# Five of nine output tiles summed on TensorE and scaled by ScalarE and GpSimd, in a new final order

## The chip, the core and the metric

The kernel runs on one core of a Trainium2 chip. The metric is the device time of one launch in microseconds, the median of several runs. Every engine has its own instruction stream and waits for others by semaphores: TensorE (PE, with its weight loads as PEld), VectorE (DVE), ScalarE (ACT), GpSimd (POOL) and SyncE (SP), which here issues nearly all the large DMAs.

## The reference: what is computed

One layer of a decoder trunk for 1024 prompt tokens and 64 sample tokens of 1024 features, all in float32. First come three parallel branches fed by one input projection, a gated sum of them and an output projection; then a mixture of experts in which each token goes to the two best of eight experts in its best group; last a normalisation. What the change touches is the last step for each token:

```python
xn2 = rmsnorm(x, n2)
x = x + hier_moe(xn2...)          # two expert outputs per token, each times its gate
...
def rmsnorm(x, g):
    y = x * rsqrt(mean(x * x) + EPS)
    return y * g
y_prompt = rmsnorm(xp, final_norm_g)
y_sample = rmsnorm(xs, final_norm_g)
```

So for each token: the residual row, plus gate 0 times the first expert's row, plus gate 1 times the second's, then the sum scaled by the inverse root of its mean square and by the gain vector.

## The kernel before

The 1088 tokens are nine tiles: 0 to 7 have 128 rows, tile 8 (the sample tokens) has 64. The program is one stream for each engine, written by hand; there is no scheduler, so that the order of the code is the order on the engine.

The first two thirds are the projections and branches (`group`, lines 2009 to 2011, three products for each to keep float32's precision). Then follow the 64 experts: their weights stream in from memory, TensorE multiplies, and GpSimd scatters each expert's rows to `ytok` in device memory (`scatter`, line 1079), so that every token finds its two rows there.

The change lies in what comes behind the last expert, which this document calls the tail. SP waits until all scatters have landed and issues nine reads, one for each tile in the order of the list `FINAL` (`load_c`, line 881); each brings both expert rows of each token into the tile's own buffer `FY[n]` (1 MB, 0.5 MB for tile 8). Then SP issues nine stores in the same order, each behind a wait for its tile (`store_c`, line 890). Reads and stores go out on one queue.

The sum of a tile is made in one of two ways:

- a tile in `WEIGHED` on TensorE: `residual` (line 2368) multiplies the residual tile `X2` by the identity into two banks of PSUM, `weigh` (line 2375) adds the two expert rows, each multiplied by a diagonal matrix `GD` of the gates. PSUM has eight banks and a tile takes two, so four tiles fit at a time. Semaphore `c_mm` tells of the sum.
- any other tile (`SUMMED`) on VectorE: `combine` (line 1970), two `scalar_tensor_tensor`, each followed by a drain, with the sum left in `X2`. Semaphore `c_sum`.

ScalarE then squares and adds up the row (`norm_f`, line 1418) and takes the root (line 1420, `c_rms`); VectorE takes the reciprocal (`norm_out`). The scaling is made in one of two ways:

- a tile in `SCALED`: ScalarE multiplies by the reciprocal (`scale_f`, line 1425, `c_scaled`), GpSimd by the gain (`gain`, line 1124, `c_gained`);
- any other (`ON_DVE`): one `scalar_tensor_tensor` on VectorE does both (line 1986, `c_out`).

ScalarE's stream puts `scale_f` of a tile behind `norm_f` of the tile that follows it in `FINAL`; VectorE's puts `norm_out` of a tile behind `combine` of the one that follows. These two rules and the lists below set the order of the tail.

```python
FINAL = [0, 3, 1, 4, 2, 5, 8, 6, 7]
WEIGHED = [3, 4, 5, 6]
SCALED = [0, 1, 2]
```

Of the kernel before, what the change touches and what calls it, by code (L numbers as in the profile page):

```python
# [9 lines left out]
ACT = mybir.ActivationFunctionType  # L10
# [10 lines left out]
NT = NFULL + 1  # L21
# [32 lines left out]
def rows_of(tile):  # L54
    return P if tile < NFULL else NDEC


def trunk(nc, x_prompt, x_sample, state_conv, state_gla, norm1_g, w_in, conv_w, gla_a2, gla_a_b,
# [17 lines left out]
    with ctx:  # L76
# [10 lines left out]
        ident = keep("ident", [P, P])  # L87
        epsc = keep("epsc", [P, 1])
# [157 lines left out]
        X2 = sb("X2", [P, NT, D])  # L246
# [84 lines left out]
        GD, = place(OH_AT, [("GD", [P, 5, 2, P])])  # L331
# [83 lines left out]
        c_mm, c_sum, c_rms, c_out, c_st = sem("c_weighted"), sem("c_sum"), sem("c_rms"), sem("c_out"), sem("c_stored")  # L415

        c_root, c_scaled, c_gained = (rms_ready, NT), (xh_ready, NT), (xl_ready, NT)
# [44 lines left out]
                eng.drain().then_inc(s_over, 1)  # L462
                eng.wait_ge(s_over, 10)

        FINAL = [0, 3, 1, 4, 2, 5, 8, 6, 7]
        WEIGHED = [3, 4, 5, 6]
        SCALED = [0, 1, 2]
        SUMMED = [n for n in FINAL if n not in WEIGHED]
        ON_DVE = [n for n in FINAL if n not in SCALED]
        T_COL = [C_V + CW * i for i in range(4)] + [C_R + CW * i for i in range(4)] + [C_VV, C_VV + CW]  # L470
        NTC = len(T_COL)
        W_R, W_LR, W_VV = 4, 7, 8
# [131 lines left out]
        def _(sp):  # L604
# [7 lines left out]
            def load_w(w):  # L612
# [287 lines left out]
        def _(pool):  # L900
# [220 lines left out]
            def gain(i):  # L1121
                out = FY[SCALED[i]][:, 0, :]
                pool.wait_ge(c_scaled[0], c_scaled[1] + i + 1)
                pool.tensor_tensor(out, out, gfb[:], ALU.mult).then_inc(c_gained[0], 1)
            pool.wait_ge(r4_in, 112)
            for i in range(len(SCALED)):
                gain(i)
# [4 lines left out]
        def _(act):  # L1132
# [276 lines left out]
            def norm_f(n):  # L1409
                rows = rows_of(n)  # L1410
                if n in WEIGHED:
                    i = WEIGHED.index(n)
                    act.wait_ge(c_mm, i + 1)
                    x2 = ps[0:rows, 2 * i:2 * i + 2, :].rearrange("p b n -> p (b n)")
                else:
                    act.wait_ge(c_sum, SUMMED.index(n) + 1)
                    x2 = X2[0:rows, n, :]
                act.activation(jf[0:rows], x2, ACT.Square, accum_out=ss6[n][0:rows])
                act.drain()
                act.activation(rt6[n][0:rows], ss6[n][0:rows], ACT.Sqrt, bias=epsc[0:rows], scale=1.0 / D).then_inc(c_rms, 1)  # L1420

            def scale_f(n):
                i = SCALED.index(n)
                act.wait_ge(c_root[0], c_root[1] + i + 1)
                act.activation(FY[n][:, 0, :], X2[:, n, :], ACT.Copy, scale=rs6[n][:]).then_inc(c_scaled[0], 1)
            for i, n in enumerate(FINAL):
                norm_f(n)
                if i and FINAL[i - 1] in SCALED:
                    scale_f(FINAL[i - 1])
# [4 lines left out]
        def _(dve):  # L1434
# [467 lines left out]
            def gate_diagonals(n):  # L1902
                rows = rows_of(n)
                i = WEIGHED.index(n)
                for k in range(2):
# [21 lines left out]
            def expert(st):  # L1927
# [22 lines left out]
                if st.n == 22:  # L1950
                    over_count()
                if st.n - 24 in WEIGHED:
                    gate_diagonals(st.n - 24)
# [20 lines left out]
            def norm_out(n):  # L1974
                rows, x2 = rows_of(n), X2[0:rows_of(n), n, :]
                dve.wait_ge(c_rms, FINAL.index(n) + 1)
                if n in SCALED:
                    dve.reciprocal(rs6[n][0:rows], rt6[n][0:rows]).then_inc(c_root[0], 1)
                    return
                dve.reciprocal(rs6[n][0:rows], rt6[n][0:rows])  # L1980
                dve.drain()
                if n in WEIGHED:
                    bank = 2 * WEIGHED.index(n)
                    dve.wait_ge(c_mm, WEIGHED.index(n) + 1)
                    x2 = ps[0:rows, bank:bank + 2, :].rearrange("p b n -> p (b n)")
                dve.scalar_tensor_tensor(out=FY[n][0:rows, 0, :], in0=x2, scalar=rs6[n][0:rows], in1=gfb[0:rows], op0=ALU.mult, op1=ALU.mult).then_inc(c_out, 1)
            for i, n in enumerate(FINAL):
                if n in SUMMED:
# [8 lines left out]
        def _(pe):  # L1997
# [48 lines left out]
            for tile in range(NT):  # L2046
                rows = rows_of(tile)
                last = pe.transpose(ps[0:LOWRANK, 4 + tile // 3, tile % 3 * P:tile % 3 * P + rows], AT[0:rows, tile, :], ident[0:rows, 0:rows])
# [313 lines left out]
                y_mul(st)  # L2362
            overflow(pe, blocks_over(pe), again)

            def residual(i):
                n, rows = WEIGHED[i], rows_of(WEIGHED[i])
                for b in range(2):
                    pe.matmul(ps[0:rows, 2 * i + b, :], ident[0:rows, 0:rows], X2[0:rows, n, b * 512:(b + 1) * 512], start=True, stop=False)

            def weigh(i):  # L2370
                n, rows = WEIGHED[i], rows_of(WEIGHED[i])
                pe.wait_ge(cy_in[n][0], cy_in[n][1] + 16)
                for b in range(2):
                    for k in range(2):
                        last = pe.matmul(ps[0:rows, 2 * i + b, :], GD[0:rows, i, k, 0:rows], FY[n][0:rows, k, b * 512:(b + 1) * 512], start=False, stop=(k == 1))
                last.then_inc(c_mm, 1)
            pe.wait_ge(y_ready, NE)
            residual(0)
            residual(1)
            for i in range(len(WEIGHED)):  # L2380
                weigh(i)
                if i + 2 < len(WEIGHED):
                    residual(i + 2)
            barrier(pe, 1)


# [26 lines left out]
```

## Time and profile before

| what | us |
|---|---|
| median of 3 runs | 1862.06 (1861.51 to 1862.4) |
| the profiled execution's own time | 1861.46 |
| its span, first to last instruction | 1859.5 |
| TensorE busy in it | 1759.5 (95%) |
| VectorE, ScalarE, GpSimd busy | 584.6, 449.3, 240.2 |
| tail: from the first read of `ytok` (1820.0) to the end | 39.5 |

The profile's page gives the busy time of each engine and the chain of work that ended last; 95% for TensorE is an average over the whole program. The tail is the last 2% of the span, and it has to be read by itself: which engine waits for which, when the reads of `ytok` land, and whether the DMA engines stand still at some point. Times in the rows count from the span's start. In a row of the timeline, the bracket at the end is the idle time of the engine before the first instruction of the row and what ended it.

### The profile page before, as it was taken

To read this page: it belongs to the slowest core of one execution; us is meant where nothing else is said; L and a number is where in the kernel's file an instruction comes from. 1 tells how busy PE (TensorE), PEld (TensorE's weight loads), DVE (VectorE), ACT (ScalarE), POOL (GpSimd) and SP (SyncE) were. 2 spreads that over 40 slices of the span, in tenths; PEclk is the share of its full clock that TensorE was granted. 3 is DMA by queue.
4 is the path that set the end of the run, shared out by engine and by line. 5 is a ranking of instruction groups with operands and counts; after the bars stand their busy time and mean duration, and the time that the engine had idled before them with its cause. 6 is when DMAs were issued, how large, how long until landed. Compare 5 with 4: busy or idle time off the path is not lost.

```text
span 1859.5 us, 27679 instructions
## 1 busy us (share of the span) xinstructions
PE 1759.5 (95%) x11544; PEld 1475.4 (79%) x11544; DVE 584.6 (31%) x1076; ACT 449.3 (24%) x802; POOL 240.2 (13%) x297
## 2 busy tenths in 40 slices
PE   8999999999999999999999999999899888888885
PEld 8999999999888888899999998887655545544442
DVE  5000102432233322255214436655333111111115
ACT  6221225632223222231122104211111111111113
POOL 0003210000001101000000000000332222222221
PEclk9999999999999999999999999999999999999998
DMA  4232223244435535267616435244899999999997
GB/s 157 94 94 96 70 85 126 95 151 141 127 114 180 167 117 169 102 215 259 227 43 236 142 94 196 93 159 161 348 421 424 425 424 424 424 425 424 424 376 294
DMA packets 159479, 406.34 MB, mean 219 GB/s; under 512 B 20342, under 2 KB 102134, under 8 KB 134779
## 3 DMA queue, kind: packets, MB, share of 16 engines
q1 hardware_dynamic: 137402, 344.22, 49.6%
q0 software_dynamic: 21952, 60.34, 8.3%
q8 instruction: 93, 1.52, 0.3%
q14 instruction: 32, 0.25, 0.0%
HBM read 340.62 MB, written 79.60 MB: 226 GB/s over the span
## 4 chain that ended last, share of the span: by engine, by line
PE 90%; issue 4%; DVE 2%; DMA 2%; ACT 1%; DVEq 0%; SPq 0%; ACTq 0%; POOLq 0%
PE ps L2009 17%; PE ps L2011 16%; PE ps L2010 16%; PE ps L2314 12%; PE ps L2207 8%; PE ps L2336 6%; PE ps L2301 2%; PE ps L2315 1%; PE ps L2325 1%; PE ps L2098 1%; PE ps L2108 1%; PE ps L2109 1%; DMA FY<-ytok 1%; PE ps L2022 1%; PE ps L2244 1%
## 5 line engine op out<-in xcount | busy, mean ns | idle before, releaser
L2009 PE MATMUL ps<-XH,WH 128*128 128x384 f32 (+1 forms) x1152 | 382.6, 332 | 0.0
L2011 PE MATMUL ps<-XH,WL 128*128 128x384 f32 (+1 forms) x1152 | 376.9, 327 | 0.0
L2010 PE MATMUL ps<-XL,WH 128*128 128x384 f32 (+1 forms) x1152 | 376.8, 327 | 0.0
L2314 PE MATMUL ps<-E,yt 128*64 128x256 f32 x1024 | 248.3, 398 | 58.8 <-issue 57.7
L2315 PE MATMUL ps<-E,yt 128*64 128x256 f32 x1024 | 249.4, 400 | 0.0
L2314 PEld LDWEIGHTS ps<-E,yt 128*64 128x64 f32 x1024 | 141.6, 143 | 120.8 <-issue 65.3
L2009 PEld LDWEIGHTS ps<-XH,WH 128*128 128x128 f32 x1152 | 216.1, 188 | 17.0 <-issue 15.1
L2010 PEld LDWEIGHTS ps<-XL,WH 128*128 128x128 f32 x1152 | 216.4, 188 | 0.0
L2011 PEld LDWEIGHTS ps<-XH,WL 128*128 128x128 f32 x1152 | 216.2, 188 | 0.0
L2009 PE MATMUL ps<-WH,XH 128*128 128x256 f32 (+2 forms) x648 | 184.3, 284 | 4.6 <-DVE XL L1450 4.6
L1456 DVE TENSOR_TENSOR WL<-RAW,WH 128x2048 fp32r<-128x2048 f32 (+1 forms) x34 | 78.1, 2298 | 347.8 <-ACT WH L1156 347.7
L2010 PE MATMUL ps<-WL,XH 128*128 128x256 f32 (+2 forms) x648 | 183.6, 283 | 0.0
L2011 PE MATMUL ps<-WH,XL 128*128 128x256 f32 (+2 forms) x648 | 183.4, 283 | 0.0
L1196 ACT ACTIVATE OF<-ps 128x384 f32<-128x384 f32 (+1 forms) x120 | 56.8, 473 | 368.8 <-PE ps L2011 368.7
L2315 PEld LDWEIGHTS ps<-E,yt 128*64 128x64 f32 x1024 | 141.8, 143 | 0.0
L2009 PEld LDWEIGHTS ps<-WH,XH 128*128 128x128 f32 (+1 forms) x648 | 122.7, 189 | 6.4 <-issue 5.6
L2336 PE MATMUL ps<-E,HT 128*64 128x512 f32 x512 | 124.0, 605 | 1.1 <-DVE HT L1924 1.1
L2011 PEld LDWEIGHTS ps<-WH,XL 128*128 128x128 f32 (+1 forms) x648 | 122.9, 190 | 0.0
L1918 DVE TENSOR_TENSOR hid<-ps,sil 64x256 f32<-64x256 f32 x64 | 26.7, 417 | 303.8 <-ACT sil L1383 303.8
L2010 PEld LDWEIGHTS ps<-WL,XH 128*128 128x128 f32 (+1 forms) x648 | 122.0, 188 | 0.0
L1079 POOL DMA_INDIRECT ytok<-YS,yidx x64 | 65.2, 1019 | 352.6 <-ACT YS L1390 352.6
L1383 ACT ACTIVATE sil<-ps 64x256 f32<-64x256 f32 x64 | 24.3, 380 | 315.0 <-PE ps L2315 315.0
(346 smaller groups left out, 2372.4 us busy)
## 6 DMA issues: line engine op xcount, KB each, us to landing
E<-in_exp_w_dram SPq DMA_DIRECT2D x192, 1024.0 KB, 27.6
RAW<-in_w_in_dram SPq DMA_DIRECT2D x29, 1024.0 KB, 7.8
feat<-OF POOLq DMA_DIRECT2D x20, 1088.0 KB, 8.0
SG<-feat SPq DMA_DIRECT2D x24, 544.0 KB, 4.8
tokd<-OT POOLq DMA_DIRECT2D x10, 1024.0 KB, 7.4
cbuf<-feat SPq DMA_DIRECT2D x16, 544.0 KB, 5.4
X<-in_x_prompt_dram SPq DMA_DIRECT2D x16, 512.0 KB, 3.5
VR<-tokd SPq DMA_DIRECT2D x32, 256.0 KB, 2.9
```

The source lines that it names most:

```text
L1079: pool.indirect_dma_start(out=ytok[:, :], out_offset=bass.IndirectOffsetOnAxis(ap=column, axis=0), in_=YS[b][:], in_offset=None, bounds_ch ...
L1196: act.activation(OF[s][:, f, t0:t0 + tn], ps[:, bank_of(w, f, g), 0:tn], func).then_inc(ev_a, 1)
L1456: dve.tensor_tensor(WL[s][:, :, 0:wd], RAW[s][:, :, 0:wd], WH[s][:, :, 0:wd].bitcast(F32), ALU.subtract).then_inc(wl_ready, 1)
L1918: dve.tensor_tensor(hid[:], ps[0:BR, 2 + st.b, 0:DE], sil[:], ALU.mult).then_inc(h_ready, 1)
L2009: pe.matmul(out, hi, mhi, start=start, stop=False)
L2010: pe.matmul(out, hi, mlo, start=False, stop=False)
L2011: return pe.matmul(out, lo, mhi, start=False, stop=stop)
L2207: last = pe.matmul(ps[:, bank + g, 0:tn], w[:, k, c], x[:, k, t0:t0 + tn], start=(k == 0 and i == 0), stop=(k == kn - 1 and i == 2))
L2301: last = pe.transpose(ps[:, b, j * P:(j + 1) * P], XG[s][:, j * P:(j + 1) * P], ident[:])
L2314: pe.matmul(ps[0:BR, 2 + b, 0:DE], XT[b][:, turned(k), :], E1[s][:, 1, k, :], start=(k == 0), stop=(k == KD - 1))
L2315: last = pe.matmul(ps[BR:P, 2 + b, 0:DE], XT[b][:, turned(k), :], E1[s][:, 0, k, :], start=(k == 0), stop=(k == KD - 1))
L2336: last = pe.matmul(ps[i * BR:(i + 1) * BR, 5 + b, :], HT[:, k, :], E2[s][:, k, i * 512:(i + 1) * 512], start=(k == 0), stop=(k == 1))
```

## The change

Three lists are new, and with them who does what:

- `FINAL` is now 0, 3, 4, 1, 5, 6, 2, 7, 8.
- `WEIGHED` has tile 7 as a fifth. It uses the two banks of the first, tile 3, so TensorE waits for VectorE's reading of tile 3's sum (`c_out`) before it writes tile 7's residual there.
- `SCALED` is now 0, 4, 1, 5, 2. The sums of tiles 4 and 5 lie in PSUM, and ScalarE reads them there.

The residual products of the first four weighed tiles now stand ahead of the first read's wait, where two did, and ScalarE takes one root of a constant before the tail begins. The change's description also speaks of the first weight chunk in halves; the diff holds no such edit, and `load_w` is as it was.

```diff
-        FINAL = [0, 3, 1, 4, 2, 5, 8, 6, 7]
-        WEIGHED = [3, 4, 5, 6]
-        SCALED = [0, 1, 2]
+        FINAL = [0, 3, 4, 1, 5, 6, 2, 7, 8]
+        WEIGHED = [3, 4, 5, 6, 7]
+        SCALED = [0, 4, 1, 5, 2]
...
+        def sum_banks(n):
+            i = WEIGHED.index(n) % 4
+            return slice(2 * i, 2 * i + 2)
...
             def scale_f(n):
                 i = SCALED.index(n)
                 act.wait_ge(c_root[0], c_root[1] + i + 1)
-                act.activation(FY[n][:, 0, :], X2[:, n, :], ACT.Copy, scale=rs6[n][:]).then_inc(c_scaled[0], 1)
+                x2 = ps[:, sum_banks(n), :].rearrange("p b n -> p (b n)") if n in WEIGHED else X2[:, n, :]
+                act.activation(FY[n][:, 0, :], x2, ACT.Copy, scale=rs6[n][:]).then_inc(c_scaled[0], 1)
+            act.activation(rt6[NT - 1][:], epsc[:], ACT.Sqrt)
+            act.drain()
...
-            residual(0)
-            residual(1)
-            for i in range(len(WEIGHED)):
-                weigh(i)
-                if i + 2 < len(WEIGHED):
-                    residual(i + 2)
+            for n in WEIGHED[:4]:
+                residual(n)
+            for i, n in enumerate(WEIGHED):
+                if i == 3:
+                    pe.wait_ge(c_out, ON_DVE.index(WEIGHED[0]) + 1)
+                    residual(WEIGHED[4])
+                weigh(n)
```

ScalarE's stream from tile 5's square to the end, before (the number behind `ss`, `rt` and `FY` is the tile's; `jf` is scratch):

```order
L1418 ACTIVATE jf,ss65<-ps 128x1024 [waits c_weighted]
L1420 ACTIVATE rt65<-ss65,epsc 128x1
L1425 ACTIVATE FY2<-X2,rs62 128x1024 [waits rms_or_final_root_ready]
L1418 ACTIVATE jf,ss68<-X2 64x1024 [waits c_sum]
L1420 ACTIVATE rt68<-ss68,epsc 64x1
L1418 ACTIVATE jf,ss66<-ps 128x1024 [waits c_weighted]
L1420 ACTIVATE rt66<-ss66,epsc 128x1
L1418 ACTIVATE jf,ss67<-X2 128x1024 [waits c_sum]
L1420 ACTIVATE rt67<-ss67,epsc 128x1
```

and in the change, from tile 6's square:

```order
L1421 ACTIVATE jf,ss66<-ps 128x1024 [waits c_weighted]
L1423 ACTIVATE rt66<-ss66,epsc 128x1
L1429 ACTIVATE FY5<-ps,rs65 128x1024 [waits rms_or_final_root_ready]
L1421 ACTIVATE jf,ss62<-X2 128x1024 [waits c_sum]
L1423 ACTIVATE rt62<-ss62,epsc 128x1
L1421 ACTIVATE jf,ss67<-ps 128x1024 [waits c_weighted]
L1423 ACTIVATE rt67<-ss67,epsc 128x1
L1429 ACTIVATE FY2<-X2,rs62 128x1024 [waits rms_or_final_root_ready]
L1421 ACTIVATE jf,ss68<-X2 64x1024 [waits c_sum]
L1423 ACTIVATE rt68<-ss68,epsc 64x1
```

The last scaling on ScalarE, tile 2's, had the squares of three tiles (8, 6, 7) behind it; it now stands behind tile 7's square and has one tile, 8, behind it.

VectorE's stream at the same place, before (`X2<-FY` is half of a sum, `rs` a reciprocal):

```order
L1970 SCALAR_TENSOR_TENSOR X2<-FY8,gates,X2 64x1024 [waits proj_or_y_in0]
L1970 SCALAR_TENSOR_TENSOR X2<-FY8,gates,X2 64x1024
L1980 RECIPROCAL rs65<-rt65 128x1 [waits c_rms]
L1986 SCALAR_TENSOR_TENSOR FY5<-ps,rs65,gfb 128x1024 [waits c_weighted]
L1980 RECIPROCAL rs68<-rt68 64x1 [waits c_rms]
L1986 SCALAR_TENSOR_TENSOR FY8<-X2,rs68,gfb 64x1024
L1970 SCALAR_TENSOR_TENSOR X2<-FY7,gates,X2 128x1024 [waits z_wo_or_y_in3]
L1970 SCALAR_TENSOR_TENSOR X2<-FY7,gates,X2 128x1024
L1980 RECIPROCAL rs66<-rt66 128x1 [waits c_rms]
L1986 SCALAR_TENSOR_TENSOR FY6<-ps,rs66,gfb 128x1024 [waits c_weighted]
L1980 RECIPROCAL rs67<-rt67 128x1 [waits c_rms]
L1986 SCALAR_TENSOR_TENSOR FY7<-X2,rs67,gfb 128x1024
```

and in the change:

```order
L1976 SCALAR_TENSOR_TENSOR X2<-FY2,gates,X2 128x1024 [waits gla_step_or_y_in2]
L1976 SCALAR_TENSOR_TENSOR X2<-FY2,gates,X2 128x1024
L1986 RECIPROCAL rs66<-rt66 128x1 [waits c_rms]
L1991 SCALAR_TENSOR_TENSOR FY6<-ps,rs66,gfb 128x1024 [waits c_weighted]
L1984 RECIPROCAL rs62<-rt62 128x1 [waits c_rms]
L1976 SCALAR_TENSOR_TENSOR X2<-FY8,gates,X2 64x1024 [waits proj_or_y_in0]
L1976 SCALAR_TENSOR_TENSOR X2<-FY8,gates,X2 64x1024
L1986 RECIPROCAL rs67<-rt67 128x1 [waits c_rms]
L1991 SCALAR_TENSOR_TENSOR FY7<-ps,rs67,gfb 128x1024 [waits c_weighted]
L1986 RECIPROCAL rs68<-rt68 64x1 [waits c_rms]
L1991 SCALAR_TENSOR_TENSOR FY8<-X2,rs68,gfb 64x1024
```

Tile 2's sum moved from the middle of the tail to the place of the third tile from the end, and tile 7's sum is gone from VectorE.

GpSimd's stream at its end, which before held the rows for tiles 0, 1 and 2 alone:

```order
L1128 TENSOR_TENSOR FY0<-FY0,gfb 128x1024 [waits xh_or_final_scaled,router_in]
L1128 TENSOR_TENSOR FY4<-FY4,gfb 128x1024 [waits xh_or_final_scaled]
L1128 TENSOR_TENSOR FY1<-FY1,gfb 128x1024 [waits xh_or_final_scaled]
L1128 TENSOR_TENSOR FY5<-FY5,gfb 128x1024 [waits xh_or_final_scaled]
L1128 TENSOR_TENSOR FY2<-FY2,gfb 128x1024 [waits xh_or_final_scaled]
```

Tiles 4 and 5 are new there, and tile 2's is the last of the five.

## Rows read from the trace of the kernel before

**Rows 1.** The page: the span.
```profile
span 1859.5 us, 27679 instructions
```
**Rows 2.** The chain of waits, tail: start us, us, what.
```profile
1822.83 18.01 DMA FY<-ytok
...
1840.88 3.71 PE ps L2375 x8
```
**Rows 3.** Stretches of the tail: us, engines' busy time, granted clock, DMA share, GB/s.
```profile
core 0: us, PE busy (x) PEld busy (x) DVE busy (x) ACT busy (x) POOL busy (x), PEclk, DMA share, GB/s
1821.00:1837.00 16.00, 9.18 (x17) 4.11 (x18) 6.65 (x7) 6.06 (x10) 0.73 (x1) 0.79 1.00 394
1837.00:1842.00 5.00, 4.54 (x11) 1.80 (x11) 4.14 (x5) 3.63 (x8) 2.28 (x2) 1.00 1.02 193
1842.00:1854.50 12.50, 6.29 (x15) 2.23 (x13) 10.42 (x12) 6.96 (x15) 4.05 (x2) 0.92 1.01 401
1854.50:1855.70 1.20, 0.00 (x0) 0.00 (x0) 1.13 (x3) 0.29 (x1) 0.00 (x0) 0.50 0.09 34
```
**Rows 4.** TensorE's timeline in the tail: start us, us, operation [idle before].
```profile
1816.84 3.70 PE L2368 MATMUL ps<-X,ident 128*128 128x512 f32 x8 [0.70 <-ACT YS L1390]
1827.83 5.74 PE L2375 MATMUL ps<-FY,GD 128*128 128x512 f32 x8 [7.28 <-DMA FY<-ytok]
...
1840.88 3.70 PE L2375 MATMUL ps<-FY,GD 128*128 128x512 f32 x8 [0.46 <-DMA FY<-ytok]
1845.99 3.70 PE L2375 MATMUL ps<-FY,GD 128*128 128x512 f32 x8 [1.41 <-DMA FY<-ytok]
```
**Rows 5.** VectorE's timeline in the tail.
```profile
1837.63 3.43 DVE L1970 SCALAR_TENSOR_TENSOR X<-FY,gates,X 128x1024 f32<-128x1024 f32 x2
1843.69 2.62 DVE L1970 SCALAR_TENSOR_TENSOR X<-FY,gates,X 64x1024 f32<-64x1024 f32 x2 [0.81 <-DMA FY<-ytok]
1848.81 1.84 DVE L1986 SCALAR_TENSOR_TENSOR FY<-X,rs,gfb 64x1024 f32<-64x1024 f32 x1
1855.09 1.28 DVE L1986 SCALAR_TENSOR_TENSOR FY<-X,rs,gfb 128x1024 f32<-128x1024 f32 x1
```
**Rows 6.** GpSimd's timeline in the tail (first and last of three).
```profile
1836.27 2.35 POOL L1124 TENSOR_TENSOR FY<-FY,gfb 128x1024 f32<-128x1024 f32 x1 [17.73 <-ACT FY L1425]
...
1847.22 2.35 POOL L1124 TENSOR_TENSOR FY<-FY,gfb 128x1024 f32<-128x1024 f32 x1 [3.52 <-ACT FY L1425]
```
**Rows 7.** ScalarE's timeline: the table load; a root, a scaling, the next square.
```profile
1829.26 1.28 ACT L1420 ACT_TABLE_LOAD   x1
...
1834.78 0.30 ACT L1420 ACTIVATE rt<-ss,epsc 128x1 f32<-128x1 f32 x1
1834.98 1.13 ACT L1425 ACTIVATE FY<-X,rs 128x1024 f32<-128x1024 f32 x1
1836.02 1.04 ACT L1418 ACTIVATE jf<-X 128x1024 f32<-128x1024 f32 x1
```
**Rows 8.** Line 881 (reads), line 890 (stores), us to landing; the last store alone.
```profile
L881 SPq DMA_DIRECT2D FY<-ytok x9: 384/526/3432, 1820.0 to 1825.5; - x9
DMA to landing us min/median/max: 5.2/13.2/23.0
L890 SPq DMA_DIRECT2D out_dram<-FY x9: 332/350/579, 1838.6 to 1856.4; - x9
out_dram<-FY SPq DMA_DIRECT2D x1, 512.0 KB, 2.6
```
**Rows 9.** Stretches with TensorE idle, and what follows: columns as in rows 3.
```profile
1557.10:1558.73 1.63, 0.00 (x1) 0.02 (x1) 0.29 (x1) 0.27 (x1) 0.56 (x1) 1.00 1.04 432
1558.89:1562.30 3.41, 3.41 (x18) 2.44 (x18) 0.00 (x0) 0.00 (x0) 1.31 (x2) 0.50 1.03 430
1540.24:1542.90 2.66, 0.01 (x1) 0.04 (x2) 0.68 (x3) 0.26 (x1) 1.29 (x2) 1.00 1.03 431
1542.90:1546.30 3.40, 3.40 (x32) 2.61 (x32) 0.00 (x0) 0.00 (x0) 0.74 (x1) 1.00 0.99 417
```

More of the change, by code:

```diff
@@ L1411, in norm_f @@
                 if n in WEIGHED:
-                    i = WEIGHED.index(n)
-                    act.wait_ge(c_mm, i + 1)
-                    x2 = ps[0:rows, 2 * i:2 * i + 2, :].rearrange("p b n -> p (b n)")
+                    act.wait_ge(c_mm, WEIGHED.index(n) + 1)
+                    x2 = ps[0:rows, sum_banks(n), :].rearrange("p b n -> p (b n)")
                 else:
@@ L1982, in norm_out @@
                 if n in WEIGHED:
-                    bank = 2 * WEIGHED.index(n)
                     dve.wait_ge(c_mm, WEIGHED.index(n) + 1)
-                    x2 = ps[0:rows, bank:bank + 2, :].rearrange("p b n -> p (b n)")
+                    x2 = ps[0:rows, sum_banks(n), :].rearrange("p b n -> p (b n)")
                 dve.scalar_tensor_tensor(out=FY[n][0:rows, 0, :], in0=x2, scalar=rs6[n][0:rows], in1=gfb[0:rows], op0=ALU.mult, op1=ALU.mult).then_inc(c_out, 1)
@@ L2363, in _, with residual, weigh @@
             overflow(pe, blocks_over(pe), again)
-            def residual(i):
-                n, rows = WEIGHED[i], rows_of(WEIGHED[i])
+            def residual(n):
+                rows, bank = rows_of(n), sum_banks(n).start
                 for b in range(2):
-                    pe.matmul(ps[0:rows, 2 * i + b, :], ident[0:rows, 0:rows], X2[0:rows, n, b * 512:(b + 1) * 512], start=True, stop=False)
-            def weigh(i):
-                n, rows = WEIGHED[i], rows_of(WEIGHED[i])
+                    pe.matmul(ps[0:rows, bank + b, :], ident[0:rows, 0:rows], X2[0:rows, n, b * 512:(b + 1) * 512], start=True, stop=False)
+            def weigh(n):
+                i, rows, bank = WEIGHED.index(n), rows_of(n), sum_banks(n).start
                 pe.wait_ge(cy_in[n][0], cy_in[n][1] + 16)
@@ L2374, in weigh @@
                     for k in range(2):
-                        last = pe.matmul(ps[0:rows, 2 * i + b, :], GD[0:rows, i, k, 0:rows], FY[n][0:rows, k, b * 512:(b + 1) * 512], start=False, stop=(k == 1))
+                        last = pe.matmul(ps[0:rows, bank + b, :], GD[0:rows, i, k, 0:rows], FY[n][0:rows, k, b * 512:(b + 1) * 512], start=False, stop=(k == 1))
                 last.then_inc(c_mm, 1)
             pe.wait_ge(y_ready, NE)
-            residual(0)
-            residual(1)
-            for i in range(len(WEIGHED)):
-                weigh(i)
-                if i + 2 < len(WEIGHED):
-                    residual(i + 2)
+            for n in WEIGHED[:4]:
[5 more added lines that the diff above has]
+                weigh(n)
             barrier(pe, 1)
```

## The prediction

> **What bounds the kernel now.** I read the page's span first [rows 1], then the chain of waits over the last 45 us, then the same stretch in windows for the DMA engines, then the timelines of the engines one by one. Everything up to the last scatter is the same code in the same order, so the question is only what the last 40 us do.
>
> There the chain stands 18 us on one item, the read of tile 5's rows [rows 2]: the tail waits for memory. The windows say how hard [rows 3]. From 1821 to 1854.5 the DMA engines are busy without a break (share 1.00 to 1.02), then comes a hole of 1.2 us at a share of 0.09, then the last two stores. Inside the busy stretch lies a slow one: from 1837 to 1842 the engines are just as busy but move 193 GB/s where 394 and 401 stand around it. I see no instruction that would explain it; it costs about 5 x (1 - 193/400) = 2.6 us. The reads land from 1820.0 + 5.2 = 1825.2 to 1825.5 + 23.0 = 1848.5 [rows 8], one megabyte each 2.5 us outside the slow stretch. Tile 5 lands at 1840.8, tile 6 at 1845.95 (TensorE waits for both) [rows 4], tile 8 at 1843.7 (VectorE waits) [rows 5]. The stores stand in the same queue behind the reads: the first is issued at 1838.6, ten microseconds before the last read has landed; the last store, alone, lands in 2.6 us [rows 8].
>
> So before the change the engines' work has little room to matter: the stores of the early tiles wait in the queue anyway, and only the hole of 1.2 us before the last two is theirs. **What the change can win is at most this hole, 1.2 us, as long as the bytes and the slow stretch stay.** It moves the same 8.5 MB in and 4.25 MB out.
>
> **The change part by part.**
>
> The residual products ahead of the reads: four more matmul pairs of the 3.70 us / 8 kind [rows 4], in TensorE's idle time between 1820.5 and 1827.8. Cover 7.3 us, cost 0. They shorten that idle time to some 3.9 us, so the granted clock, which was 0.50 for most of tile 3's weighing (5.74 us against 3.70 for the others [rows 4]), may stay up. That makes tile 3's sum up to 2.0 us earlier; what comes next on its way is the store, which waits in the queue until the reads are through: worth 0 at the end.
>
> The early root on ScalarE takes the 1.28 us table load [rows 7] out of tile 0's way. Tile 0's store waits in the same queue: 0.
>
> Tile 7's sum goes from VectorE (2.62 us) to TensorE (3.70 us) [rows 4, 5]; its wait for tile 3's output is over long before, since VectorE has that between 1835 and 1837 and TensorE asks at 1839. Behind this wait stand the weighings of tiles 6 and 7 only.
>
> Scaling of tiles 4 and 5: two `scalar_tensor_tensor` of 1.28 us leave VectorE, two scalings of 1.04 us in ScalarE's stream [rows 7] and two gains of 2.35 us on GpSimd [rows 6] are added. The form that scales from PSUM does not stand in the trace. Its bounds are the nearest rows of the same size: 1.04, the square on ScalarE, and 1.28, a `scalar_tensor_tensor` on VectorE; I take the 1.13 of the old scaling [rows 5, 7]. The difference of 0.15 us at most, once on the path, is inside the range.
>
> **What this adds up to is a new order of arrival at the end.** The reads, by their position in bytes (the old landings are at 6 MB 1840.8, 6.5 MB 1843.7, 7.5 MB 1845.95, 8.5 MB 1848.5): tile 6 at 1840.8, tile 2 at 7 MB 1844.8, tile 7 at 8 MB 1847.2, tile 8 at 1848.5. Tile 2, which still takes the longest way (VectorE sum, ScalarE square and root, ScalarE scaling, GpSimd gain), now arrives seventh instead of fifth.
>
> Step by step for tile 2:
> - its two half sums on VectorE start at 1844.8. GpSimd's gains for tiles 1 and 5 run then: scaling of tile 1 ends at about 1844.1, so 1844.2 to 1846.6; tile 5's from about 1847.3 (behind tile 6's square and root, which ends at 1846.1) to 1849.6.
> - VectorE pays for these. In the old trace the half sum that began under a gain (1837.63, gain until 1838.62) made the pair last 3.43 instead of 2.62; and tile 8's scaling, begun at 1848.81 under the gain until 1849.57, lasted 1.84 instead of 1.28 [rows 5, 6]. Both fit one reading: the VectorE operation ends about 1.08 us after GpSimd's. So the first half ends at 1846.6 + 1.08 = 1847.7, the second at 1849.6 + 1.08 = 1850.7. Without this they would be done at 1847.5.
> - ScalarE: square and root 1.2 + 0.3 (1850.8 to 1852.3). The next in its stream is tile 7's square and root, ready since 1847.2 + 3.7 = 1850.9: 1852.2 to 1853.6. Only then tile 2's scaling, 1.13: 1854.7.
> - GpSimd's gain 2.35 with the hand-over: 1854.9 to 1857.2. Store issued at 1857.25.
> - the stores of tiles 7 and 8 stand behind it in SP's stream, so nothing is left that could use the queue. The six stores before it end by about 1855.7, and the DMA engines stand still again. From the issue: 2.6 us for the first [rows 8], then 1.25 us for tile 7 (0.52 MB at the 401 GB/s of rows 3 is 1.3) and 0.63 for tile 8: 1861.75. Old last landing: 1856.4 + 2.6 = 1859.0. The end moves by +2.7; the same arithmetic run over the old order ends 0.1 too late, so +2.6.
>
> Span 1859.5 + 2.6 = 1862.1; with the 1.96 us that lie between span and time of the profiled execution (1861.46 - 1859.5), 1864.1. That execution is 0.6 below the median of the runs shown, 1862.06; I stay with the sum from the trace. It is 0.11% above the median: within the 0.2% (3.7 us) that a measurement of this kernel can tell from no change.
>
> Bounds of the unknown price, VectorE beside GpSimd. None: tile 2's sum is done at 1847.5, ScalarE turns to tile 7 at 1850.9, the scaling ends at 1853.5, the store is issued at 1856.0: 1862.9. Both ways, so that GpSimd also waits for a half sum that began first (0.4 at tile 5's gain, 0.6 at tile 2's): 1864.7. I take the middle, since the rows show VectorE stretched and GpSimd's three at 2.35 each.
>
> The Trainium skill says more than the rows (SBUF — State Buffer, "SBUF: two separate sides"): a VectorE operation with two SBUF inputs and a GpSimd operation take one shared port pair as an exclusive lock, whichever comes first, and the other blocks fully. The two stretched rows agree with the blocking of VectorE; no row shows GpSimd blocked. By that rule the time is the upper of the two bounds, 1864.7, and it speaks against this change, which goes from three gains to five.
>
> **The rivals.**
>
> The lock both ways, 1864.7 (bound above). For it: GpSimd's gains for tiles 5 and 2 would begin in the middle of a half sum, which no old gain did. Against it: no row shows it.
>
> Without the stretching, 1862.9 (bound above). For it: a gain that starts some tenths later than I have it misses the half sums. Against it: two gains almost back to back leave little room.
>
> The slow stretch of 1837 to 1842 is missing. For it: nothing in the program explains it, and the rest of the expert stage shows 417 to 432 GB/s [rows 9]. Against it: the unprofiled runs lie within 0.9 us of each other and the profiled one, which has it, below all, so it is no accident of one run. Without it the reads end 2.6 to 4 us earlier, but the chain through ScalarE and GpSimd gives only part back: by the same steps the span is 1858.4 to 1859.2, the time 1860.4 to 1861.2. If the engines' chain also kept up, the transfers alone would bound: 1859.0 - 1.2 - 2.6 - their waits of about 1, some 1856 to 1857, faster by over 0.2%.
>
> Slower beyond 0.2%: the clock. TensorE stands idle from 1844.6 to 1847.2 in front of tile 7's weighing, where before the last sum was VectorE's. In the expert stage the granted clock was down to 0.50 after 1.6 us of idleness (1557.10) but stayed at 1.00 after 2.66 (1540.24) [rows 9]. Where it falls before 1847.2, the weighing takes twice 3.7 = 7.4 us, and its square, tile 2's scaling behind it and the three stores come later: 1864.7 for the span, 1866.7 for the time. It decides from a weighing longer than about 5 us; half of it at the low clock (5.5 us) gives 1864.8.
>
> That the change does not do what it says: the halves of the first weight chunk are not in it, so the first 40 us stay as they are, for a gain of 0.
>
> **How the numbers follow.** Forecast 1864.1, 0.33. The lock both ways, 1864.7: 0.15. Without stretching, 1862.9: 0.17. No slow stretch, 1860.8: 0.18. Low clock, 1866.7: 0.11. Transfers alone, 1856.5: 0.06. The range from 1860.6 to 1866.4 takes in the price's bounds and most of the third case. Slower by over 0.2% (above 1865.8): the clock's 0.11 and a tail of the forecast, 0.15. Faster (below 1858.3): 0.06. Within: 0.79.
>
> **What would show it.** In the new profile: a hole in the DMA share between 1854 and 1858 longer than 1.2 us; tile 2's store issued last but two, near 1857, ended by GpSimd; VectorE's half sums of tile 2 longer than 1.28 each, ended 1.08 after a gain; a GpSimd operation longer than 2.35 or late would show the lock both ways. Tile 7's weighing at 3.7 us clears the clock. Wrong would be: the DMA share at 1.0 to the end (then the transfers bind and the time is at or under 1861), or a 1837-like stretch that is absent or has moved.

## The result and the profile after

The changed kernel takes 1866.32 us (median of 12 runs, 1864.91 to 1867.04), the kernel before 1862.05 in the same comparison (12 runs, 1861.49 to 1862.69). The ratio is 1.0023 with a 95% interval of 1.0016 to 1.0031: slower by 4.3 us. The profiled execution took 1866.31.

The page's first line answers [rows 1]:

```profile
span 1864.1 us, 27702 instructions
```

4.6 us longer. The first read of `ytok` starts at 1820.18 (1819.98 before), so 4.4 of them lie in the tail: 43.97 us against 39.56.

TensorE's timeline in the tail (start us, us, operation, idle before) answers [rows 4]:

```profile
1817.03 7.13 PE L2373 MATMUL ps<-X,ident 128*128 128x512 f32 x16 [0.70 <-ACT YS L1394]
1828.21 13.39 PE L2380 MATMUL ps<-FY,GD 128*128 128x512 f32 x24 [4.05 <-DMA FY<-ytok]
1841.43 1.88 PE L2373 MATMUL ps<-X,ident 128*128 128x512 f32 x4
1843.15 7.30 PE L2380 MATMUL ps<-FY,GD 128*128 128x512 f32 x16
```

The residuals of four tiles stand in one row, as the change says. The row of 24 products is tiles 3, 4 and 5: 13.39 us, where three times 3.70 would be 11.1. The chain of waits says where the difference is (start us, us, what):

```profile
1820.60 7.57 DMA FY<-ytok
1828.21 6.53 PE ps L2380 x8
1834.77 1.02 ACT jf L1421
...
1836.52 1.28 DVE FY L1991
1837.80 3.08 DVEq L1977
1840.96 1.28 DVE X L1976
1842.35 1.06 ACT jf L1421
...
1844.87 1.00 ACT jf L1421 x2
...
1846.43 1.95 DVEq L1977
1848.45 3.21 DVE X L1976
...
1852.07 1.28 DVE FY L1991
...
1855.03 1.28 DVE X L1976
...
1858.19 1.41 DVE FY L1991
```

Before, this chain stood 18 us on the read of tile 5 [rows 2]; now it leaves memory at 1828.2 and goes through the engines to the end. Its first link is tile 3's weighing, 6.53 us. Its two longest VectorE links (L1977 is the drain behind the first half sum, L1976 a half sum) lie beside gains. The windows give the clock of that weighing (columns as in [rows 3]):

```profile
1828.21:1833.90 5.69, 5.69 (x7) 2.53 (x8) 0.29 (x2) 1.44 (x3) 0.00 (x0) 0.50 1.02 413
1834.00:1837.00 3.00, 3.00 (x8) 1.33 (x7) 0.65 (x2) 2.16 (x4) 0.00 (x0) 1.00 1.02 404
```

Granted 0.50, so 1.2 GHz, after 4.05 us of idleness. VectorE's timeline answers [rows 5]:

```profile
1836.52 1.28 DVE L1991 SCALAR_TENSOR_TENSOR FY<-ps,rs,gfb 128x1024 f32<-128x1024 f32 x1
1837.72 4.52 DVE L1976 SCALAR_TENSOR_TENSOR X<-FY,gates,X 128x1024 f32<-128x1024 f32 x2
...
1846.35 5.32 DVE L1976 SCALAR_TENSOR_TENSOR X<-FY,gates,X 128x1024 f32<-128x1024 f32 x2
...
1853.40 2.90 DVE L1976 SCALAR_TENSOR_TENSOR X<-FY,gates,X 64x1024 f32<-64x1024 f32 x2
```

Tile 1's pair (1837.72) stands in VectorE's stream behind the scaling of tile 3 and starts only when that is done, just under tile 0's gain; it takes 4.52 us, tile 2's pair 5.32, where 2.62 is the pair alone [rows 5]. GpSimd's timeline, and its five gains in one line (min/median/max in ns), answer [rows 6]:

```profile
1837.44 2.36 POOL L1128 TENSOR_TENSOR FY<-FY,gfb 128x1024 f32<-128x1024 f32 x1 [18.71 <-ACT FY L1429]
1844.94 8.93 POOL L1128 TENSOR_TENSOR FY<-FY,gfb 128x1024 f32<-128x1024 f32 x3 [5.14 <-ACT FY L1429]
1855.77 2.74 POOL L1128 TENSOR_TENSOR FY<-FY,gfb 128x1024 f32<-128x1024 f32 x1 [1.90 <-ACT FY L1429]
...
L1128 POOL TENSOR_TENSOR FY<-FY,gfb x5: 2356/2744/3327, 1837.4 to 1855.8; 128x1024 f32<-128x1024 f32 x5
```

The gains of tiles 4, 1 and 5 stand back to back for 8.93 us, 2.98 each on average instead of 2.35: GpSimd is held up as well. The scaling that reads PSUM takes 1.10 us on ScalarE. The windows of the DMA engines answer [rows 3]:

```profile
1837.00:1842.00 5.00, 5.00 (x13) 2.22 (x12) 4.93 (x3) 1.70 (x4) 2.36 (x1) 1.00 1.02 410
1842.40:1846.00 3.60, 3.60 (x10) 1.60 (x9) 0.33 (x2) 3.46 (x7) 1.06 (x1) 1.00 1.03 258
1846.00:1854.00 8.00, 4.45 (x10) 1.44 (x8) 7.42 (x7) 5.72 (x10) 7.82 (x3) 1.00 0.53 217
1853.20:1854.40 1.20, 0.00 (x0) 0.00 (x0) 1.20 (x3) 1.13 (x4) 0.68 (x1) 1.00 0.00 0
1857.40:1859.40 2.00, 0.00 (x0) 0.00 (x0) 1.93 (x3) 0.46 (x3) 1.12 (x1) 0.50 0.03 10
```

Once the reads are through, the share falls to 0.53, then to nothing twice: the stores wait for the engines. The slow stretch is still there, but five microseconds later than in [rows 3]. The last read lands at 1847.97, 27.8 us after the first is issued, where it was 28.5; tile 2's rows land at 1842.46. The nine stores (line 894, to [rows 8]) are issued from 1839.8 to 1859.6; tile 2's goes out at 1858.54, and the last has landed at 1863.63.

### The profile page after: what moved, and what is told of

Read it like the earlier page. It is cut to its first block, busy times and chain, and to the rows that moved or that the text cites. A ratio compares the mean times of both kernels' runs of the same rounds, so it can differ in the third digit from the quotient of the medians.

```text
span 1864.1 us, 27702 instructions
## 1 busy us (share of the span) xinstructions
PE 1763.8 (95%) x11556; PEld 1479.4 (79%) x11556; DVE 582.7 (31%) x1074; ACT 451.8 (24%) x805; POOL 247.4 (13%) x299
## 4 chain that ended last, share of the span: by engine, by line
PE 90%; issue 4%; DVE 3%; DMA 2%; DVEq 1%; ACT 1%; SPq 0%; ACTq 0%; POOLq 0%
PE ps L2014 17%; PE ps L2016 16%; PE ps L2015 16%; PE ps L2319 12%; PE ps L2212 8%; PE ps L2341 6%; PE ps L2306 2%; PE ps L2320 1%; PE ps L2330 1%; PE ps L2103 1%; PE ps L2113 1%; PE ps L2114 1%; PE ps L2027 1%; PE ps L2249 1%; DMA SG<-feat 1%
## 5 line engine op out<-in xcount | busy, mean ns | idle before, releaser
L2319 PE MATMUL ps<-E,yt 128*64 128x256 f32 x1024 | 243.4, 393 | 63.4 <-issue 62.5
L2320 PE MATMUL ps<-E,yt 128*64 128x256 f32 x1024 | 244.6, 394 | 0.0
L2319 PEld LDWEIGHTS ps<-E,yt 128*64 128x64 f32 x1024 | 139.6, 141 | 122.6 <-issue 69.1
L2320 PEld LDWEIGHTS ps<-E,yt 128*64 128x64 f32 x1024 | 139.6, 141 | 0.0
```

The costliest lines, as they stand in the source:

```text
L2319: pe.matmul(ps[0:BR, 2 + b, 0:DE], XT[b][:, turned(k), :], E1[s][:, 1, k, :], start=(k == 0), stop=(k == KD - 1))
L2320: last = pe.matmul(ps[BR:P, 2 + b, 0:DE], XT[b][:, turned(k), :], E1[s][:, 0, k, :], start=(k == 0), stop=(k == KD - 1))
```

## The experiments

My theory (A) after this reading: the tail is a chain through the engines. The low clock of tile 3's weighing starts it, VectorE's stream hands the delay to tile 1's sum and from there to all tiles behind it, and GpSimd's gains and VectorE's half sums lengthen each other. Where an expectation gives theories letters, A is this chain. The rivals: one link alone carries the loss (the number of gains, the new order, the fifth weighed tile, or the early residuals), or the transfers do. Differences are against the kernel before on the same chip. They are not to be added, since links of one chain overlap. An interval is about 1.7 us to either side, so two kernels of the table whose differences lie closer than some 2 us are not told apart by their times. A tail is that of one execution, and the ratio is not exactly the quotient of the two medians.

| kernel | median us | against before, us | ratio (95%) | tail in the profile, us |
|---|---|---|---|---|
| before | 1861.4 to 1862.1 | | | 39.6 |
| the change | 1866.32 | +4.3 | 1.0023 (1.0016 to 1.0031) | 44.0 |
| e1 | 1866.03 | +4.2 | 1.0024 (1.0015 to 1.0033) | 43.7 |
| e2 | 1861.36 | -0.5 | 1.0000 (0.9991 to 1.0009) | 39.1 |
| e3 | 1865.49 | +3.6 | 1.0020 (1.0011 to 1.0029) | 42.8 |
| e4 | 1863.85 | +2.0 | 1.0011 (1.0002 to 1.0020) | 41.6 |
| e5 | 1863.44 | +1.9 | 1.0013 (1.0004 to 1.0022) | 40.6 |
| e6 | 1866.08 | +4.5 | 1.0023 (1.0014 to 1.0033) | 44.6 |
| e7 | 1864.54 | +3.0 | 1.0011 (1.0002 to 1.0020) | 42.3 |
| e8 | 1861.23 | -0.3 | 1.0000 (0.9991 to 1.0009) | 38.3 |
| f1 | 1863.35 | +1.9 | 1.0013 (1.0004 to 1.0022) | 41.0 |
| f2 | 1863.26 | +1.8 | 1.0008 (0.9999 to 1.0017) | 40.6 |
| f3 | 1862.19 | +0.7 | 1.0000 (0.9991 to 1.0009) | 38.3 |
| f4 | 1868.21 | +6.8 | 1.0036 (1.0022 to 1.0049) | 43.9 |

**e1, the change with eight products more, to fill TensorE's idle time.**

```diff
-            for n in WEIGHED[:4]:
+            for n in WEIGHED[:3]:
                 residual(n)
+            for _ in range(8):
+                pe.matmul(ps[:, 6, :], ident[:], X2[:, 6, 0:512], start=True, stop=True)
+            residual(WEIGHED[3])
```

> The changed kernel with eight more 128x512 products (3.5 us) in TensorE's idle time before the first weighing; their result is overwritten and used nowhere. Theory A (the chain from tile 3's weighing over tile 1's sum on VectorE sets the tail, and the low clock there is part of it): the weighing of tile 3 takes 3.7 us instead of 6.5, everything behind it on VectorE comes 2.7 us earlier, and the time falls by 0.8 to 2.8 us, to 1863.5 to 1865.5. Theory B (the transfers set the end): 1866.3, no change.

Inconclusive, by my sizing. TensorE's timeline:

```profile
1822.91 7.03 PE L2386 MATMUL ps<-X,ident 128*128 128x512 f32 x16
...
1831.49 10.46 PE L2380 MATMUL ps<-FY,GD 128*128 128x512 f32 x24
```

Each product is two rows of 0.43 us here; I had counted one, so they lasted 7.03 us instead of 3.5. The clock stayed up (24 products in 10.46 us), but the weighing began at 1831.49, after tile 3's rows had landed (1830.09). f1 repeats it in the right size.

**f1, the same with three products.**

```diff
-            for n in WEIGHED[:4]:
+            for n in WEIGHED[:3]:
                 residual(n)
+            for _ in range(3):
+                pe.matmul(ps[:, 6, :], ident[:], X2[:, 6, 0:512], start=True, stop=True)
+            residual(WEIGHED[3])
```

> The changed kernel with three more 128x512 products (2.6 us, each two passes of 0.43) in TensorE's idle time before tile 3's weighing, so that they end before its rows land; their result is used nowhere. The eight of the first try took 7.0 us and held the weighing back by 2.2. Theory A (tile 3's weighing at half clock is the first link of the chain): weighing 3.7 us instead of 6.5 and the time 2.7 us lower, 1863.6; at least 1 us lower. Theory B (its clock costs nothing at the end, as the prediction had it): 1866.3.

TensorE's timeline and the window of tile 3's weighing:

```profile
1821.59 2.74 PE L2386 MATMUL ps<-X,ident 128*128 128x512 f32 x6
...
1827.32 7.13 PE L2380 MATMUL ps<-FY,GD 128*128 128x512 f32 x16 [1.28 <-DMA FY<-ytok]
```

```profile
1827.32:1831.00 3.68, 3.68 (x9) 1.77 (x10) 0.30 (x2) 1.44 (x3) 0.00 (x0) 1.00 1.02 413
```

As theory A had it: tiles 3 and 4 in 7.13 us at a granted clock of 1.00, the tail 3.0 us shorter than the change's, the difference to the kernel before 1.9 instead of 4.3. So 2.4 us of the change's time by the medians, 3.0 by the tails of one execution each, hang on the low clock of one weighing of 3.7 us. The half sums under the gain are still long (tile 1's pair 4.51 us), which is part of what remains.

**e2, the change with gains of one column, the rest of those five tiles left without the gain.**

```diff
-                pool.tensor_tensor(out, out, gfb[:], ALU.mult).then_inc(c_gained[0], 1)
+                pool.tensor_tensor(out[:, 0:1], out[:, 0:1], gfb[:, 0:1], ALU.mult).then_inc(c_gained[0], 1)
```

> The changed kernel, where GpSimd multiplies only the first of 1024 columns of the five scaled tiles by the gain (the other columns of these tiles are left without it). Waits and order are the same. Theory A (VectorE and GpSimd block each other, and the last gain is on the path): VectorE's half sums are all back at 1.3 us, the time falls by 4 us, to 1862.3. Theory B (transfers or the clock alone): 1865.5 to 1866.3.

The gains, and the half sums of the change and of e2 in a line each (ns, min/median/max):

```profile
L1128 POOL TENSOR_TENSOR FY<-FY,gfb x5: 189/191/311, 1837.1 to 1853.3; 128x1 f32<-128x1 f32 x5
...
L1976 DVE SCALAR_TENSOR_TENSOR X<-FY,gates,X x8: 1258/1280/1284, 1826.5 to 1852.2; 128x1024 f32<-128x1024 f32 x6, 64x1024 f32<-64x1024 f32 x2
```

```profile
L1976 DVE SCALAR_TENSOR_TENSOR X<-FY,gates,X x8: 1277/1420/3214, 1825.7 to 1855.0; 128x1024 f32<-128x1024 f32 x6, 64x1024 f32<-64x1024 f32 x2
```

Without gains no half sum is longer than 1284 ns, and the time is that of the kernel before, though the clock in tile 3's weighing is still low. So the low clock alone does not make the loss: it needs the gains behind it. This kernel also leaves out the gains' own length, 2.74 us of it at the very end of the change, so it does not separate that from the holding.

**e4, the change with tile 1's sum ahead of tile 3's scaling on VectorE.**

```diff
-                if n in SUMMED:
+                if n in SUMMED and n != 1:
                     combine(n)
+                if FINAL[i] == 4:
+                    combine(1)
                 if i:
                     norm_out(FINAL[i - 1])
```

> The changed kernel with tile 1's sum on VectorE moved ahead of tile 3's reciprocal and scaling, so that it no longer waits for TensorE's first sum. Theory A: tile 1's sum is done at about 1836 instead of 1842.2 and the chain behind it moves up: -1.7 us, 1864.6. Theory B (transfers): 1866.3.

```profile
1832.97 2.64 DVE L1976 SCALAR_TENSOR_TENSOR X<-FY,gates,X 128x1024 f32<-128x1024 f32 x2 [3.16 <-DMA FY<-ytok]
...
1843.21 5.33 DVE L1976 SCALAR_TENSOR_TENSOR X<-FY,gates,X 128x1024 f32<-128x1024 f32 x2
```

Tile 1's pair starts when its rows land (1832.97 against 1837.72) and lasts 2.64; 2.3 us of the loss go (theory A: 1.7), with the clock as low as in the change. The link between weighing and tile 1's sum is VectorE's stream, as theory A has it.

**e3, the change with three scaled tiles.** `SCALED = [0, 1, 2]`; tiles 4 and 5 go back to VectorE.

> The changed kernel with ScalarE and GpSimd scaling tiles 0, 1 and 2 alone, as before the change; tiles 4 and 5 are scaled on VectorE. Theory A: two gains fewer block VectorE less, but two operations of 1.28 us are back on it: -1.2 us, 1865.1. If the gains are the whole cost: 1862.5. If only the clock and the order cost: 1866.3.

```profile
L1128 POOL TENSOR_TENSOR FY<-FY,gfb x3: 2355/2362/2452, 1837.9 to 1855.7; 128x1024 f32<-128x1024 f32 x3
```

Only 0.6 us better (1.2 in the tail), although the gains are short again: close to theory A's 1865.1 and far from 1862.5, but too little to be told from no change. I read it so that VectorE gets back as work what tiles 4 and 5 spare GpSimd. The number of gains is not the loss in itself; that tile 2 takes the long way so late stays in this kernel.

**e5, the kernel before with the early residuals and the early root.**

```diff
+            act.activation(rt6[NT - 1][:], epsc[:], ACT.Sqrt)
+            act.drain()
...
-            residual(0)
-            residual(1)
+            for i in range(4):
+                residual(i)
             for i in range(len(WEIGHED)):
                 weigh(i)
-                if i + 2 < len(WEIGHED):
-                    residual(i + 2)
```

> The kernel before with two parts of the change alone: all four residual products ahead of the first weighing, and the early root on ScalarE. Every theory: no change, 1862.0 to 1862.1; if the table load or the residuals stood on the path, up to 1.3 us faster.

```profile
1828.74 8.82 PE L2377 MATMUL ps<-FY,GD 128*128 128x512 f32 x16 [3.92 <-DMA FY<-ytok]
1841.14 9.01 PE L2377 MATMUL ps<-FY,GD 128*128 128x512 f32 x16 [3.58 <-DMA FY<-ytok]
```

The residuals ahead do not keep the clock up in tile 3 (8.82 us for tiles 3 and 4). They also take work away from between the weighings: TensorE now stands idle for 3.58 us ahead of tile 5 and weighs 5 and 6 in 9.01 us, where before each took 3.70 [rows 4]. In the old order this part alone costs 1.9 us (1.1 in the tail), which no theory had. That the residuals do it and not the early root, which is in this kernel too, is read from this timeline and not tested.

**e6 and e7, the old order with five scaled tiles, and with five weighed tiles** (both with the early residuals).

```diff
-        FINAL = [0, 3, 4, 1, 5, 6, 2, 7, 8]
-        WEIGHED = [3, 4, 5, 6, 7]
-        SCALED = [0, 4, 1, 5, 2]
+        FINAL = [0, 3, 1, 4, 2, 5, 8, 6, 7]
+        WEIGHED = [3, 4, 5, 6]
+        SCALED = [0, 1, 4, 2, 5]
...
-                if i == 3:
-                    pe.wait_ge(c_out, ON_DVE.index(WEIGHED[0]) + 1)
-                    residual(WEIGHED[4])
```

> The old final order and four weighed tiles, with tiles 4 and 5 scaled on ScalarE and GpSimd as in the change (and the early residuals and root). Theory A (five gains block VectorE): +2.3 us, 1864.3. If the gains cost nothing and the order of arrival is the whole loss: 1862.1.

In e7 the lists are `WEIGHED = [3, 4, 5, 6, 7]` and `SCALED = [0, 1, 2]`, and the three lines of the loop stay.

> The old final order and the three old scaled tiles, with tile 7 summed on TensorE as in the change (and the early residuals and root). VectorE is relieved of 2.6 us in front of the last two stores. If the transfers bind with their slow stretch: 1862.2. If the engines bind: 2.6 us faster, 1859.4. If the fifth weighed tile is what costs in the change: over 1863.

e6's gains, then e7's weighing of tile 5:

```profile
L1128 POOL TENSOR_TENSOR FY<-FY,gfb x5: 2345/2790/3267, 1836.7 to 1852.3; 128x1024 f32<-128x1024 f32 x5
```

```profile
1841.49 6.58 PE L2380 MATMUL ps<-FY,GD 128*128 128x512 f32 x8 [3.31 <-DMA FY<-ytok]
```

Both lose in the old order too (4.5 and 3.0 us, 1.9 of each is e5's share if that carries over). What is then left of e6, 2.6, is near theory A's 2.3. What is left of e7, 1.1, is inside its interval, and its 11 runs lie between 1859.52 and 1867.02, so a cost of the fifth weighed tile is not shown. The new order is not the sole cause.

**e8, no tile scaled by ScalarE and GpSimd.** Five weighed, VectorE scales all nine, tile 8 is read first.

```diff
-        FINAL = [0, 3, 4, 1, 5, 6, 2, 7, 8]
-        SCALED = [0, 4, 1, 5, 2]
+        FINAL = [8, 3, 0, 4, 1, 5, 2, 6, 7]
+        SCALED = []
```

> Five weighed tiles, no gain on GpSimd at all (VectorE scales all nine tiles), the half tile 8 first, and the order 8, 3, 0, 4, 1, 5, 2, 6, 7. Theory A: nothing blocks VectorE, the store queue never runs empty, and the time is that of the transfers: 1858.1 without the slow stretch, 1862.1 with it. If scaling on VectorE is what costs: over 1863.

The same time as before, within 0.09%, and a tail 1.3 us shorter; theory A's two times, 1858.1 and 1862.1, lie to either side of it. A kernel without GpSimd's help is no slower here: nine scalings of 1.28 us fit on VectorE once no gain holds it. The clock is low in tile 3's weighing here too (tiles 3 and 4 take 10.04 us). Since tile 8's place and the order of tiles 2 and 6 were changed with it, e8 does not say what the gains cost by themselves.

**f2, the kernel before with tile 8's read first** (the stores stay in their order).

```diff
+            load_c(8)
             for n in FINAL:
-                load_c(n)
+                if n != 8:
+                    load_c(n)
```

> The kernel before, with the read of tile 8 (64 partitions) issued first and all else in its order. In every profile so far the slow stretch of the transfers lay where tile 8's read stood in the queue. Theory C (tile 8's read to 64 partitions is the slow stretch): the stretch moves from 17 to 22 us after the first read to 1 to 5 us, and the last read lands up to 2 us earlier. Theory D (the stretch belongs to a place in memory or to tile 5): it stays where tile 5 is read. For the time: tile 0 lands 2 us later and its gain falls on other half sums, so 1861.5 to 1863.5 by theory A.

```profile
1822.30:1825.40 3.10, 0.00 (x0) 0.00 (x0) 0.00 (x0) 0.00 (x0) 0.00 (x0) 0.66 1.02 237
...
1837.40:1842.40 5.00, 5.00 (x13) 2.12 (x12) 3.93 (x5) 3.63 (x8) 2.36 (x1) 1.00 1.02 406
```

The slow stretch follows tile 8's read, as theory C has it: from 1822.3 there are 237 GB/s, and the five microseconds that had 193 [rows 3] have 406. The last read lands 26.9 us after the first is issued instead of 28.5. That gave no gain in time (+1.8 us, and the interval begins at 0.9999); every other tile now comes later at the start, which I take for the reason and did not test.

**f3, what the experiments point to: e8 with f1's three products,** tile 8 first, tile 6 ahead of tile 2.

```diff
-        FINAL = [8, 3, 0, 4, 1, 5, 2, 6, 7]
+        FINAL = [8, 3, 0, 4, 1, 5, 6, 2, 7]
...
-            for n in WEIGHED[:4]:
+            for n in WEIGHED[:3]:
                 residual(n)
+            for _ in range(3):
+                pe.matmul(ps[:, 6, :], ident[:], X2[:, 6, 0:512], start=True, stop=True)
+            residual(WEIGHED[3])
```

> The version that the runs so far point to: tile 8 first, five weighed tiles, all scaling on VectorE, order 8, 3, 0, 4, 1, 5, 6, 2, 7, and the three filling products. By theory A the transfers bind alone: tail of 37.5 to 38.3 us from the first read, against 39.6 before, and a time of 1860.0 to 1861.2. If the low clock in the last weighing returns: 1862 or more.

```profile
1827.76 3.70 PE L2380 MATMUL ps<-FY,GD 128*128 128x512 f32 x8 [0.67 <-DMA FY<-ytok]
```

```profile
1825.00:1854.40 29.40, 21.78 (x49) 8.68 (x47) 22.53 (x26) 12.71 (x27) 0.00 (x0) 1.00 1.01 404
```

The clock is up in every weighing and the DMA engines move 404 GB/s without a break. The profiled tail is 38.3 us, 1.3 below that of before, yet the median is 0.7 above with an interval of 0.9991 to 1.0009. Its 11 runs spread from 1857.86 to 1862.97, and the profiled one, at 1860.58, is 1.6 below their median. The stretch ahead of the tail, nearly the same work in every kernel here, varies too: over the 14 profiles the first read is issued between 1819.48 and 1821.04. A gain of 1.3 us in one tail is no larger than that. No kernel here beats the one before measurably; whether the 1.3 us are there in the other runs stays open.

**f4, the change with two residuals back between the weighings.**

```diff
-            for n in WEIGHED[:4]:
+            for n in WEIGHED[:2]:
                 residual(n)
...
                 weigh(n)
+                if i < 2:
+                    residual(WEIGHED[i + 2])
```

> The changed kernel with the residual products of the third and fourth weighed tile put back between the weighings, as before the change. If the early residuals cost something by themselves (idle time between weighings that lets the clock fall): 0.5 to 1.5 us faster than the change, 1865. If they are free, as the prediction had it: 1866.3, or slightly slower, since 1.7 us of products stand in front of the weighings of tiles 4 and 5.

```profile
1828.57 5.34 PE L2380 MATMUL ps<-FY,GD 128*128 128x512 f32 x8 [7.32 <-DMA FY<-ytok]
1833.75 1.88 PE L2373 MATMUL ps<-X,ident 128*128 128x512 f32 x4
```

I expected it 0.5 to 1.5 us faster than the change; it was slower (five runs, 1866.73 to 1869.47), with a profiled tail as long as the change's (43.9). Tile 3's weighing is 1.2 us shorter, but tile 4's residual of 1.88 now stands behind it. In this order, then, the early residuals are not what hurts, unlike in e5. Tile 2's gain begins 0.5 us sooner after the first read than in the change, but takes 3.18 us instead of 2.74, held by a half sum of tile 8. The profiled execution, 1866.73, is the fastest of the five, and this kernel was not timed beside the change; whether its time is truly the longer one stays open.

## Where the prediction was right, which step failed, and what was luck

The forecast was 1864.1, the measured time 1866.32: inside the range to 1866.4 by less than 0.1 us, but slower beyond 0.2%, to which I gave 0.15. The loss is 4.3 us where 2.0 were forecast.

*Tile 2 arrives seventh, the stores of 7 and 8 behind it: right.* The prediction had its store last but two, issued at 1857.25; it was 1858.54. It had a hole in the DMA share longer than the old 1.2 us; there are two, 1.2 and about 2 us.

*The half sums of tile 2 end 1.08 us behind a gain: right in kind.* The gains were those of tiles 4 and 1, not of 1 and 5: they end at 1847.30 and 1850.59, the half sums at 1848.38 and 1851.67. Forecast end 1850.7. They began at 1846.35, not at 1844.8: ahead of them in VectorE's stream stands tile 5's reciprocal, whose root waited on ScalarE behind tile 4's scaling, behind tile 1's square, behind tile 1's late sum.

*"Tile 3's sum up to 2.0 us earlier ... worth 0 at the end": this step failed.* The clock did not stay up; the weighing took 6.53 us, 0.8 longer than before. And it was priced at nothing because I followed tile 3 itself to its store. What stands behind tile 3's scaling in VectorE's stream is tile 1's sum, and that is on the path. f1 measures the term at 2.4 to 3.0 us, e4 the link at 2.3; a forecast of 1864.1 plus 2.4 would have been 1866.5. That this meets the measured time so well is part luck, by the next step.

*Tile 2's rows land at 1844.8, behind the slow stretch: wrong, and it hid part of the failed step.* They landed at 1842.46 and lay there for 3.9 us. Had VectorE been free at once, the pair would have begun 2.3 us ahead of the forecast. With the clock kept (f1) it begins 23.1 us after the first read, where the forecast has 24.8 and the change 26.2, and the tail is 41.0 us, where the forecast has 42.1 (1862.1 - 1820.0) and the change 44.0. So the forecast's tail was 1.1 us longer than the same chain with the clock kept, and the term priced at nothing left out 3.0.

*The price of VectorE beside GpSimd: I took the middle, and the upper bound was right.* The rival "lock both ways" said that a GpSimd operation longer than 2.35 us would show it: three of five are (3.23, 3.33 and 2.74), and the last of them comes straight onto the end. Each of the three ends 2.21 us behind the half sum that stood before it (1848.38 and 1850.59, 1851.67 and 1853.88, 1856.31 and 1858.52). The Trainium skill (SBUF — State Buffer, "SBUF: two separate sides") had stated it: the pair of ports goes to whichever starts first, and the other blocks fully. With that rule the trace agrees in both directions, 3.21 us for a half sum and 3.33 for a gain. I had made 1864.7 of it; my two terms, 0.4 and 0.6, add up to 1865.1 if both stand on the path. Either way it does not cover the rest.

*The low clock in tile 7's weighing: wrong.* TensorE itself was late: it began tile 6 at 1843.15 and weighed 6 and 7 in 7.30 us without a break. The low clock was a rival, but in the wrong place.

*The slow stretch: kept in the sum, unexplained, and I gave 0.18 to its absence.* It is tile 8's read, of 64 partitions (f2); the change moved that read to the end of the queue, and the stretch with it. The reads were through 0.7 us sooner after the first issue (27.8 for 28.5), but the engines set the end, so nothing came of it.

*The early root and the scaling from PSUM at 1.13: right within 0.03 us.*

Of the 2.0 us between the forecast span (1862.1) and the measured (1864.1), 1.0 is the later sum, 0.4 the last gain's 2.74 instead of 2.35, and 0.6 lies in the three stores, which take 5.1 us from the first issue where I had 4.5 (tile 2's at 1858.54, the end at 1863.63). Two thirds of that 0.6 is tile 8's store of 0.25 MB: it lands 1.04 us behind tile 7's, where I had 0.63 by the full rate. Another 0.2 is between span and time (2.2 in this execution, 1.96 before).

## What to carry to other kernels

A late result on one tile is priced by what stands behind its wait in the stream of the waiting engine, not by its own way to the store. A product moved out of an idle stretch can leave another long enough to halve the clock of the work that follows, so read the idle time ahead of every block again after such a move. When two-input VectorE work and GpSimd work share a tail, moving work to GpSimd does not unload VectorE; a kernel that leaves GpSimd out and reads tile 8 first took the same time as the one before.

## What the runs showed of the hardware

**A read of 64 partitions about halves the rate while its turn in the queue lasts.** 193 to 258 GB/s at a share of 1.02 to 1.03, against 394 to 410 around it, in every kernel at the place of tile 8's read (17 to 22 us after the first read in the old order, 22 to 26 in the new, 1 to 5 where it stands first). The Trainium skill (SBUF — State Buffer, "Door 1: The DMA port swizzle (why `[64,N]` ≈ `[32,N]`)") says that the 16 DMA ports are picked by bits of the partition number, so that partitions 0 to 63 reach only half of them. The rate, about half, agrees; no run here used other partitions. The store of tile 8 fits too: 0.25 MB in 1.04 us behind tile 7's 0.5 MB in 1.31 is 252 against 400 GB/s.

**One small instruction fetch, one late landing.** In the change one fetch of 0.02 MB stands in the window of 1834 to 1837 (DMA queues: packets, MB, share):

```profile
q8 instruction: 1, 0.02, 2.3%
```

The next read of 1 MB then lands 4.06 us behind the one ahead of it instead of 2.56, and those behind it make nothing up, while the rate stays at 404 GB/s. In e1 and f1 the fetch comes at other times (1827.5 and 1833.9) and the gap goes with it (4.01 and 3.95). All 14 profiles have one such fetch in the reads, between 6.7 and 19.1 us after the first is issued, and in all of them the first landing behind it is late, 3.87 to 5.40 us behind the one ahead. In the kernel before it falls together with tile 8's read: at 1836.5, and tile 5's rows, the 18 us of [rows 2], land 5.40 us behind those ahead of them. In f2 the two are apart: 237 GB/s at tile 8's read, and a gap of 4.00 us at the fetch with 406 GB/s around it. No run removed the fetch, so that it is the cause is read, not shown.

**VectorE's scaling from PSUM does not wait for a gain.** Tile 6's scaling, which reads its sum in PSUM and the gain vector in SBUF, ran at 1852.07 in 1.28 us in the middle of a gain (1850.55 to 1853.88), and that gain ended 2.21 us behind the half sum ahead of it, as the others did. What gains held were half sums and tile 8's scaling, whose two inputs both lie in SBUF.

**The clock after idleness.** A weighing of 3.70 us took 6.53 after 4.05 us idle, 6.58 after 3.31 (e7), 5.34 after 7.32 (f4) and 3.70 after 0.67 and after 2.78 (f3); f1 kept 1.00 after 1.28. The longest idle time did not cost the most.
